# A two-layer decoder step: the key cache of the second head group turned by VectorE instead of TensorE

## The reference

```
ATT_GROUPS = ((128, 1), (512, 4), (2048, 16))        # window, dilation
k_all = jnp.concatenate([c[:, :, 0], k[:, :, gi]], axis=1)
idx = n_past + jnp.arange(t)[:, None] - j[None, :] * dil
kg = k_all[:, idx].astype(jnp.float32)
sc = jnp.einsum('bthd,btjhd->bhtj', q.astype(jnp.float32), kg) * (HEAD_DIM ** -0.5)
```

## Time and profile before

| | before |
|---|---|
| median of 3 runs | 1919.84 us (1918.83 to 1922.17) |
| the profiled execution | 1915.48 us |
| its span, first to last instruction | 1913.6 us |
| PE busy | 1877.8 us (98%) |
| DVE, ACT, POOL busy | 638.8, 460.9, 193.3 us |
| granted PE clock, mean | 0.996 |
| one DMA issue of a chunk on SP | 0.37 us |
| bytes moved by DMA | 553.82 MB, mean 289 GB/s |

### The profile page before, as it was taken

One profiled execution on the slowest core, in us unless ns is written; L12 is line 12 of the kernel. 1 busy time (PEld: TensorE's weight loads), 2 busy tenths in 40 slices (PEclk: granted clock), 3 DMA queues, 4 the chain that ended last, 5 costly groups with the idle time before them and its releaser, 6 DMA issues.

```text
span 1913.6 us, 44783 instructions
## 1 busy us (share of the span) xinstructions
PE 1877.8 (98%) x20479; PEld 1282.5 (67%) x20480; DVE 638.8 (33%) x1081; ACT 460.9 (24%) x688; POOL 193.3 (10%) x260
## 2 busy tenths in 40 slices
PE   8999999999999999999999999999999999999998
PEld 8998877999999998877874353534435353443535
DVE  5456543654434556643541010110201011020101
ACT  5434442444424444443431000000000000000000
POOL 2114100233403113200100000000000000000000
PEclk9999999999999999999999999999999999999999
DMA  9443799655545443689547999999999999999996
GB/s 300 144 154 123 234 310 358 202 160 159 172 158 185 152 144 130 211 287 356 187 160 265 415 383 409 404 383 409 373 415 386 404 407 382 410 375 415 385 405 267
DMA packets 212399, 553.82 MB, mean 289 GB/s; under 512 B 11482, under 2 KB 107914, under 8 KB 195680
## 3 DMA queue, kind: packets, MB, share of 16 engines
q1 hardware_dynamic: 208864, 541.71, 76.7%
q0 software_dynamic: 3248, 9.18, 1.4%
q10 hardware_dynamic: 96, 0.02, 0.0%
HBM read 543.46 MB, written 7.77 MB: 288 GB/s over the span
## 4 chain that ended last, share of the span: by engine, by line
PE 95%; DVE 2%; DMA 1%; ACT 1%; issue 1%; SPq 0%; DVEq 0%; POOL 0%; ACTq 0%; POOLq 0%
PE psum L952 89%; PE psum L960 6%; DMA low_part<-in_w_branch_attn 1%; DVE w_split L1823 1%; ACT w_split L1544 0%; DMA low_part<-in_x_sample 0%; DVE low_part L2322 0%; DVE low_part L1816 0%; DVE low_part L1935 0%; DVE high_part L1940 0%; ACT low_part L1514 0%; DVE high_part L1860 0%; DVE xn_split L1835 0%; SPq L814 0%; DVE xn_tok L2186 0%
## 5 line engine op out<-in xcount | busy, mean ns | idle before, releaser
L952 PE MATMUL psum<-low_part 128*32 128x512 f32 (+3 forms) x6926 | 675.2, 526 | 6.8 <-ACT low_part L1514 4.8
L952 PEld LDWEIGHTS psum<-xn_split,w_split 128*128 128x128 f32 x3744 | 502.8, 188 | 36.7 <-issue 31.0
L952 PE MATMUL psum<-xn_split,w_split 128*128 128x288 f32 x3744 | 519.4, 297 | 1.5 <-DVE w_split L1823 1.3
L952 PEld LDWEIGHTS psum<-low_part 128*32 128x32 f32 (+2 forms) x6926 | 239.9, 114 | 398.0 <-issue 390.1
L952 PE MATMUL psum<-low_part,high_part 128*32 128x256 f32 (+3 forms) x6636 | 343.3, 359 | 3.4 <-DVE low_part L1816 2.3
L1823 DVE TENSOR_TENSOR w_split<-low_part,w_split 128x2048 fp32r<-128x2048 f32 x104 | 238.7, 2296 | 267.0 <-ACT w_split L1544 266.8
L952 PEld LDWEIGHTS psum<-low_part,high_part 128*32 128x32 f32 (+1 forms) x6636 | 217.0, 111 | 129.2 <-issue 14.9
L1544 ACT ACTIVATE w_split<-low_part 128x2048 fp32r<-128x2048 f32 x104 | 199.1, 1914 | 264.8 <-PE psum L952 216.7
L2334 DVE TENSOR_TENSOR low_part<-high_part,psum 128x384 f32<-128x384 f32 (+1 forms) x48 | 29.8, 621 | 426.2 <-PE psum L952 423.8
L1787 ACT ACTIVATE high_part<-psum 128x384 f32<-128x384 f32 (+1 forms) x48 | 25.9, 544 | 395.0 <-PE psum L952 394.1
L960 PE MATMUL psum<-high_part,low_part 128*128 128x128 f32 (+2 forms) x839 | 109.8, 281 | 10.1 <-DMA low_part<-in_x_sample 6.9
(11 more groups left out here) (159 smaller groups left out, 942.7 us busy)
## 6 DMA issues: line engine op xcount, KB each, us to landing
low_part<-in_we_down SPq DMA_DIRECT2D x112, 1024.0 KB, 8.5
low_part<-in_cache_kv_g SPq DMA_DIRECT2D x72, 1024.0 KB, 5.7
low_part<-in_we_gate SPq DMA_DIRECT2D x64, 1024.0 KB, 8.2
low_part<-in_we_up SPq DMA_DIRECT2D x64, 1024.0 KB, 8.6
low_part<-in_w_in SPq DMA_DIRECT2D x55, 1024.0 KB, 5.1
low_part<-in_we_gate SPq DMA_DIRECT2D x64, 768.0 KB, 7.7
low_part<-in_we_up SPq DMA_DIRECT2D x64, 768.0 KB, 7.3
low_part<-in_w_dense SPq DMA_DIRECT2D x33, 1024.0 KB, 5.4
```

The costliest lines, as they stand in the source:

```text
L952: signal(e.matmul(out, lhsT, rhs, start=start, stop=stop, skip_group_check=mixed), inc)
```

## The change

Chunks of the nine types now alternate between groups 1 and 2. The eight of group 1 (four a half) are "by quarters": a chunk is loaded by four DMAs, each into 32 partitions, so that partition block i holds heads 2i and 2i + 1, its 128 keys cut in four runs of 32. One DVE instruction then turns every 32x32 block of the chunk into `keysT` (two buffers that share their place with `cacheT`), and PE scores it from there. Its queries are placed to match, by eight small copies each on ACT and DVE (`place_quarters`), at the ends of units 1 and 5. The chunks of groups 0 and 2 are turned by PE as before, two tiles in a slot (half a unit), and ACT makes all their copies. All but the last three chunks are scored within the units, one in a slot, from slot 3 on; half 1 begins within the units, its score bank is now bank 6, and its tiles go through bank 7 alone. POOL places the rows of half 1 between its scalings (`place_queries`) and after them (`place_far`). Half 0's softmax is taken after the units, behind the split of the first gate chunk, whose load goes ahead of the last two key chunks.

```diff
-KPOOL, ST_BANKS, O_BANKS, UPOOL, UKPOOL = (0, 1, 2, 3), (5, 4), (6, 7), (0, 1, 2, 3, 4), (6, 7)
+KPOOL, SS_BANKS, O_BANKS, UPOOL, UKPOOL = (0, 1, 2, 3), (5, 6), (7, 6), (0, 1, 2, 3, 4), ((6, 7), (7,))
+KEY_TYPES = [(0, None)] + [(g, t) for t in range(DS) for g in (1, 2)]
+def by_quarters(n):
+    return KEY_TYPES[n][0] == 1
+KEY_SLOTS = 2 * (NU + 1)
+KEYS_FROM = 3
+ROWS_AT = 4
+QUARTERS_AT = (1, (KEYS_FROM + NQ - 2) // 2)
+def key_steps():
+    out = [[] for _ in range(KEY_SLOTS + 1)]
+    for q in range(HB * NQ):
+        half, n = divmod(q, NQ)
+        at = KEYS_FROM + q
+        out[min(at, KEY_SLOTS)].append(("score", half, n))
+        for b in range(BH if not by_quarters(n) else 0):
+            out[min(at - 2 + b // 2, KEY_SLOTS)].append(("turn", half, BH * n + b))
+    for steps in out[:KEY_SLOTS]:
+        steps.sort()
...
+    out[KEY_SLOTS] = [score[0], turn[0], turn[1], score[1], turn[2], turn[3], score[2]]
...
+    keys = ["C"] * (N_CACHE // 2)
+    keys.insert(GATE_AHEAD, steps[0])
...
+                    if c in QUARTERED:
+                        dst = view(slot(c), BH, 4, 128)
+                        src = src.rearrange("(k s) b (i d) -> i s b k d", k=4, i=4)
+                        send(L, c, [(dst[QUAD * i:QUAD * (i + 1)], src[i]) for i in range(4)])
...
+                    if quarters:
+                        e.wait_ge(quarters_placed.sem, quarters_placed.at(L, 16 * (half + 1)))
+                        e.wait_ge(keys_turned.sem, keys_turned.at(L, half * DS + (q % NQ + 1) // 2))
+                    else:
+                        if n0:
+                            e.wait_ge(rows_placed.sem, rows_placed.at(L, 16 * (half + 1)))
...
+                        if (half, n) == (1, NQ - 1):
+                            turn_s_probs(0)
+                        score_chunk(half * NQ + n)
...
+                        cache_copies(2 * v + he)
                         if v + 1 < NU:
                             soften(2 * (v + 1) + he)
...
+                    if v in QUARTERS_AT:
+                        half = QUARTERS_AT.index(v)
+                        wait_quarters(e, L, half)
+                        place_quarters(lambda out, in_: e.activation(out, in_, ACT.Copy), half, 0)
...
+                split_high(L, W_MERGE)
+                cache_copies(KEY_SLOTS)
+                sample_exp(e, L, 0)
+                place_probs(e, L, S, 0)
...
+                def turn_keys(q):
+                    c = CACHE_CHUNK[q]
+                    wait_chunk(e, L, c)
+                    e.wait_ge(split_used, L * NW_LAYER + W_MERGE)
+                    wait_cache_slot(e, L, S, BH * q)
+                    e.transpose(keysT[L][q % 2].rearrange("p b k x s -> p (b k x s)"), view(slot(c), CH))\
+                        .then_inc(keys_turned.sem, 1)
...
+                split_low(L, W_MERGE)
+                softmax_bias(0)
+                softmax_scale(0)
+                new_probs(0)
...
+                place_queries(e, L, 0)
+                place_far(e, L, 0)
                 for u in range(2 * ACT_SCALED, 2 * NU):
                     scale(u)
+                    if u == 2 * ROWS_AT + 1:
+                        e.wait_ge(scored.sem, scored.at(L, 1))
+                        place_queries(e, L, 1)
+                S.wait_full(e, ("ss", 0))
+                place_far(e, L, 1)
```

More of the change, by code:

```diff
@@ L184 @@
 K_STORES = [(g, tt) for g in range(G) for tt in range(3) if (g, tt) != (0, 0)]
+KEY_TYPES = [(0, None)] + [(g, t) for t in range(DS) for g in (1, 2)]
+def by_quarters(n):
+    return KEY_TYPES[n][0] == 1
 def cache_tiles():
[L189 to L193, removed]
+    return [(n, b, g, b, t) for n, (g, t) in enumerate(KEY_TYPES) for b in range(BH)]
 TILES = cache_tiles()
@@ L199 @@
 CACHE_SLOTS = 8
[L202 to L215, removed]
+KEY_SLOTS = 2 * (NU + 1)
[12 more added lines that the diff above has]
+        steps.sort()
+    last = out[KEY_SLOTS]
+    score = [x for x in last if x[0] == "score"]
+    turn = [x for x in last if x[0] == "turn"]
+    assert len(score) == 3 and len(turn) == BH
+    out[KEY_SLOTS] = [score[0], turn[0], turn[1], score[1], turn[2], turn[3], score[2]]
+    return out
+KEY_STEPS = key_steps()
+TURNED_AHEAD = [[NQ * half + n for kind, half, n in KEY_STEPS[at + 1] if kind == "score" and by_quarters(n)]
+                for at in range(KEY_SLOTS)]
 SCORES_AT = 32
 K_HOMES = 4
-MAX_AT, EXP_AT, SCALE_AT, PT_AT = 3, 6, 9, 14
 EX0_GATE = 4
@@ L251, in branch_tiles, with key_jobs @@
     return [(name, 2 * i + x) for x in range(2) for name in ("pb", "ab")]
+def key_jobs(at):
+    out = []
+    for kind, half, n in KEY_STEPS[at]:
+        if kind == "turn":
+            out.append((("kT", half, n), UKPOOL[half] if at < KEY_SLOTS else KPOOL))
+        elif n == 0:
+            out.append((("ss", half), (SS_BANKS[half],)))
+    return out
 def section_attention():
@@ new lines, in place_queries, with place_far @@
+        def place_queries(e, L, half):
+            rows = q_all.rearrange("p (g j) b t h -> p g j (b t) h", g=G)
+            for he in range(2):
+                p = slice(64 * he, 64 * he + 64)
+                for j in range(J):
+                    e.tensor_copy(rows[p, :, j, :, 2 * j + he], new_queries(half)[p, :, j, :]).then_inc(rows_placed.sem, 1)
+                e.wait_ge(rows_placed.sem, rows_placed.at(L, 16 * half + 4 * he + 4))
+        def place_far(e, L, half):
+            for he in range(2):
+                p = slice(64 * he, 64 * he + 64)
+                one = view(q_one_at + J * BH * DS * 32, J * BH * DS * 32)[p, :]
+                for j in range(J):
+                    e.tensor_copy(strided(one, j * BH * DS * 32 + 2 * j + he, (128, BH), (32 + H, DS)),
+                                  new_queries(half)[p, 2, j, :].rearrange("p (b t) -> p b t", b=BH)).then_inc(rows_placed.sem, 1)
+                e.wait_ge(rows_placed.sem, rows_placed.at(L, 16 * half + 4 * he + 12))
@@ new lines, in wait_quarters, with place_quarters @@
+        def wait_quarters(e, L, half):
+            if half == 0:
+                e.wait_ge(zeroed.sem, zeroed.at(L, 1))
+            else:
+                e.wait_ge(scored.sem, scored.at(L, NQ - 1))
+        def place_quarters(copy, half, he):
+            for j in range(J):
+                one = view(q_one_at, J * BH * DS * 32)[QUAD * j:QUAD * (j + 1), :]
+                for x in (2 * he, 2 * he + 1):
+                    copy(strided(one, x * BH * DS * 32 + 2 * j + he, (128, BH), (32 + H, DS)),
+                         new_queries(half)[QUAD * x:QUAD * (x + 1), 1, j, :].rearrange("p (b t) -> p b t", b=BH))\
+                        .then_inc(quarters_placed.sem, 1)
@@ L1230, in attention @@
                         scores(v + 1)
[L1231 to L1232 removed]
+                    key_steps_at(2 * v)
                     if v == 1:
```

151 lines of the change are left out of this document (59 added, 92 removed).

## The result

The changed kernel takes 1930.93 us (median of 7 runs, 1926.0 to 1934.26) against 1918.83 us of the kernel before (7 runs): a ratio of 1.0055 over all the runs (the two medians alone give 1.0063), interval 1.0036 to 1.0073. It is 0.55% slower. The time lies at the upper edge of the range that was given (1908 to 1931), and the forecast was no change. The profiled execution took 1931.60 us, 16.1 more than that of before.

The account below looks back on a forecast made before the run. PE (TensorE), busy 98% of the span, was taken as the bound; 18.7 us removed against 18.2 added a layer gave -1.0 in all, so 1918.9 us and no measurable change, range 1908 to 1931.

Parts of the forecast that it names:

- What is removed: Per layer, 8 x 16 transposes leave PE (16.2 us) and two later PE waits go (2.5 us): together -18.7 us.
- One bank: Half 1's tiles, bank 7 alone: nine waits for ACT's copy at 0.98 us, 8.8 a layer; last chunk 0.8 more.
- Rows for half 1: Half 1's second chunk needs `place_far`, on POOL behind all units' scaling: PE waits 3.3 us a layer.
- Probabilities of half 0: Made only at the end, on DVE behind the first gate chunk's split: PE waits 3.1 us a layer.
- Queries by quarters: In unit 1 ACT places its eight query copies last: PE waits 2.2 us a layer; in unit 5, nothing.
- Start: Stage start: PE turns four tiles inside today's 2.4 us wait; change taken as 0, ends -1 and +1.
- The sum: Per layer 18.2 us added on PE against 18.7 taken away: -0.5 a layer, -1.0 us in all.
- The turning by VectorE: DVE turns each 128x2048 chunk in some 2.29 us, covered beside PE's work, so taken at nothing.
- The loads: Quartered chunk loads into 32 partitions: 5.4 us each taken, range 2.7 to 10.8, all hidden up to 8.3.
- Rival 3: Slower: quartered loads bind if a chunk takes over 8.3 us; at 10.8, 15 us a layer, 1949; chance 0.12.
- Rival 1: Faster: ACT keeps up, so bank places and long waits are shorter; -10.4 us in all, 1909.4; chance 0.26.
- Rival 2: Slower: PE's clock falls with its waits, about 1.5 us a spell; five more give 1926.4; chance 0.22.

## Why the prediction was wrong

- *What is removed.* Right: 256 transposes in all, and the unit at 7.07 us against 7.1.
- *One bank.* Right: nine places a layer, the second tile 1.37 to 1.41 after the first, so 0.94 to 0.98 each against 0.98, and 0.84 for the chunk behind slot 17 against 0.8.
- *Rows for half 1.* 2.8 against 3.3 (its own terms give 3.4). *Probabilities of half 0.* 2.8 and 2.3 against 3.1. *Queries by quarters.* 1.5 and 1.7 against 2.2, but here the spell ahead of it made PE late: in the run with filled gaps, at the full clock, PE's own work ends at 765.16 and the chunk starts at 767.50, 2.3 later. *Start.* 2.6 and 2.4 of waits against the 2.4 of before, so 0 as taken. So of the three long ones two came out 10 to 26% shorter (POOL's eight copies, for one, took 1.30 us and not 1.4), the third as forecast.
- *The sum.* Right: the forecast was 88.7 us for the stage, at the full clock; the run with filled gaps has 88.5 and 88.3 (its added waits: 8.7 + 0.8 + 2.8 + 2.8 + 2.3 = 17.4, against 18.2), and its 1916.6 us stand against the 1918.9 forecast.
- *The turning by VectorE.* 2.31 us against 2.29, and PE doesn't wait for it. *The loads.* About 5.2 us a chunk against 5.4, hidden; DVE's turning waits for scorings of PE, not for DMAs. Rival 3 did not come, though it was near: it binds as soon as the stage is 14 us shorter.
- *Rival 1.* ACT did not make up for the bank waits: 17.4 and 16.9 us of waits in the two layers. Nor do all the added waits end with ACT's queue, as the rival had it: that for the rows ends with POOL (L835), that for the probabilities with DVE (L2126).
- *Rival 2* is what happened, with more of it than was allowed. The step that failed is the one that costed each wait at its length, at a clock of 1.00, and left the clock to a rival at 0.22. Its price of 1.5 us a spell was near (a window of 8 us with 0.79 has lost 1.7), but its count was not: I reckoned with one spell for a long wait in two, and not at all for the bank waits. The windows of layer 0 hold the loss of six such steps instead of one. Against the run with filled gaps the clock cost 7.9 and 8.6 us in the two stages, 17.0 in the profiled executions (1931.6 against 1914.6) and 14.4 by the medians. That price is measured; for which gap each spell came is not shown. The argument against the rival, 1.00 over layer 1's stage in the earlier trace rows, was from a stage with one long wait and 83.6 of 89.2 us busy; the changed one has five long and ten short waits, and PE busy for some 70 us if the clock holds (83.6 less the transposes' 14 to 16).

## What to carry to other kernels

Where PE is the bound, work that is moved off it is worth only what the waits in its place leave, and a wait costs more than its length: here 17 us of waits in a stage of 88 cost another 8 at the lower clock, though not wait by wait: filling one or nine of them gave nothing clear of the spread, filling all of them 14 us. So sum the waits of a new order before anything else, and add for the clock by the rows of the profile that show it. To tell the clock from all else, fill PE's gaps with idle work of the kind that was removed, see in the trace that it stands in the gap and not behind it, and take the time again; and take the waits away one by one, the long ones first, asking of each bank that you free whose copy comes last.

## What the runs showed of the hardware

That a kernel gains by doing useless work: 141 idle transposes a layer made it 14 us faster (1930.9 to 1916.6). That PE can be busy without a break and be granted half the clock: 52 passes of 32 columns took 11.30 us with the clock at 0.50; what such work lacks, no row tells. That a spell can come behind two waits of under 1 us (799.40 in the run with the long gaps filled), and also with PE busy for all of the 8 us and no wait above 0.3 in the 10 before: 304 to 312 in the changed kernel, 176 to 184 in the run with the long gaps filled, 0.79 each. And that the spells differ from one execution to the next: the kernel with the start filled ran from 1919.1 to 1933.6 us, and its mean clock went with the time.
